# Memory's token tiles: turned by VectorE's block transposes and 128-byte stores, in place of TensorE

## What is computed

```python
h = rmsnorm(x, norm_mix_w)
gq, gk, gv, ggate, ga, dq, dk, dv, dgate = split_cols(h @ w_in)
o_gla = gla_chunked(gq, gk, gv, g)              # gated linear attention, 4 heads
o_diff = diff_attention(q, k, dv, lam)          # two softmax maps, 4 heads
x = x + concat(o_gla, o_diff) @ w_out
hc = rmsnorm(x, norm_cross_w)
mem_n = rmsnorm(mem, norm_mem_w)                # (256, 1024): the change is here
kv = mem_n @ w_ckv                              # keys and values of the memory
x = x + cross_attention(hc, kv, w_cq, w_co)
return rmsnorm(x, final_norm_w)
```

## Time and profile before

| | us |
|---|---|
| median of 3 runs | 816.72 |
| lowest to highest | 815.28 to 817.65 |
| the profiled execution's own time | 814.48 |
| its span, first to last instruction | 812.7 |
| TensorE busy in the span | 799.4 (98%) |
| VectorE busy | 593.1 (73%) |
| ScalarE busy | 422.1 (52%) |
| mean granted TensorE clock | 0.998 |

### The profile page before, as it was taken

How to read it: one execution, slowest core, us unless ns; L and a number is a source line. 1 busy time by engine, 2 the same in 40 slices (tenths; PEclk the granted TensorE clock), 3 DMA queues, 4 the chain that set the end, 5 groups by cost and what they waited for, 6 DMA issues and landing times.

```text
span 812.7 us, 13040 instructions
## 1 busy us (share of the span) xinstructions
PE 799.4 (98%) x4376; PEld 669.9 (82%) x4376; DVE 593.1 (73%) x1386; ACT 422.1 (52%) x1025; POOL 98.8 (12%) x138
## 2 busy tenths in 40 slices
PE   8999999999999999999999999999999999999996
PEld 7887888888788888888888798888888888888885
DVE  6688677675678678767868877798847563367997
ACT  7766445444455345445535556543645553366453
POOL 3100111121011010111212211010010000001201
PEclk9999999999999999999999999999999999999999
DMA  8331236568365334545667368954457312107945
GB/s 283 128 84 40 85 98 170 97 111 156 66 111 112 87 95 114 108 81 98 126 132 162 108 173 269 317 125 124 146 134 177 102 66 74 57 14 153 215 86 207
DMA packets 126538, 103.41 MB, mean 127 GB/s; under 512 B 58628, under 2 KB 96648, under 8 KB 126472
## 3 DMA queue, kind: packets, MB, share of 16 engines
q1 hardware_dynamic: 98184, 66.40, 28.2%
q0 software_dynamic: 15392, 29.36, 20.1%
q10 hardware_dynamic: 12896, 6.82, 2.9%
HBM read 85.77 MB, written 33.55 MB: 147 GB/s over the span
## 4 chain that ended last, share of the span: by engine, by line
PE 83%; DVE 9%; ACT 4%; issue 2%; DMA 1%; POOL 0%; ACTq 0%; DVEq 0%
PE bank L1936 14%; PE bank L1938 14%; PE bank L1937 14%; PE banks2to L1936 9%; PE banks2to L1938 9%; PE banks2to L1937 9%; PE banks2to L2193 3%; PE banks6to L1999 3%; PE bank L2216 2%; DVE w_lo L1442 2%; DVE neg_max L1738 1%; DVE actT_lo L1441 1%; PE banks2to L2133 1%; PE bank L2218 1%; PE banks2to L2120 1%
## 5 line engine op out<-in xcount | busy, mean ns | idle before, releaser
L1938 PE MATMUL bank<-w_hi,actT_lo 128*128 128x512 f32 x412 | 161.5, 392 | 0.0
L1936 PE MATMUL bank<-w_hi,actT_hi 128*128 128x512 f32 x384 | 154.6, 403 | 0.5 <-DVE memT_lo L1441 0.2
L1937 PE MATMUL bank<-w_lo,actT_hi 128*128 128x512 f32 x384 | 149.8, 390 | 0.0
L1442 DVE SCALAR_TENSOR_TENSOR w_lo<-w_raw,vecs,w_hi 128x512 fp32r<-128x512 f32 x120 | 87.0, 748 | 24.1 <-ACT w_hi L1158 23.8
L1938 PEld LDWEIGHTS bank<-w_hi,actT_lo 128*128 128x128 f32 x412 | 77.4, 188 | 16.9
L1158 ACT ACTIVATE w_hi<-w_raw,vecs 128x512 fp32r<-128x512 f32 x120 | 83.1, 721 | 14.3 <-DMA w_raw<-in_w_ckv 8.7
L1936 PEld LDWEIGHTS bank<-w_hi,actT_hi 128*128 128x128 f32 x384 | 72.2, 188 | 16.7 <-DVE w_lo L1442 1.6
L1937 PEld LDWEIGHTS bank<-w_lo,actT_hi 128*128 128x128 f32 x384 | 72.4, 188 | 13.1
L1030 POOL TENSOR_TENSOR rs_o<-var_o,neg_half 128x1 f32<-128x1 f32 (+1 forms) x48 | 31.1, 647 | 343.8 <-DVE var_o L1766 228.5
L1938 PE MATMUL banks2to<-w_hi,actT_lo 128*128 128x512 f32 x164 | 64.0, 390 | 0.0
L1325 ACT ACTIVATE prob<-banks2to,neg_maxs 128x128 f32<-128x128 f32 (+7 forms) x64 | 46.9, 740 | 15.2 <-DVE neg_maxs L1739 15.0
(11 more groups left out here) (377 smaller groups left out, 2037.6 us busy)
## 6 DMA issues: line engine op xcount, KB each, us to landing
w_raw<-in_w_in SPq DMA_DIRECT2D x56, 256.0 KB, 3.0
out_sums<-in_w_out POOLq DMA_DIRECT2D x11, 1024.0 KB, 9.0
late_sums<-in_w_co POOLq DMA_DIRECT2D x11, 1024.0 KB, 9.2
w_raw<-in_w_ckv SPq DMA_DIRECT2D x32, 256.0 KB, 3.6
w_raw<-in_w_cq SPq DMA_DIRECT2D x32, 256.0 KB, 2.9
stage_in<-in_x SPq DMA_DIRECT2D x8, 512.0 KB, 4.6
mixT<-mixed ACTq DMA_DIRECT2D x16, 256.0 KB, 4.0
x_res<-in_x SPq DMA_DIRECT2D x8, 512.0 KB, 5.7
```

The lines of the kernel that those rows point to most:

```text
L1442: return dve.scalar_tensor_tensor(dst, src, scale, hi.bitcast(F32), ALU.mult, ALU.subtract)
L1936: pe.matmul(dst, l_hi, r_hi, start=start, stop=False)
L1937: pe.matmul(dst, l_hi, r_lo, start=False, stop=False)
L1938: return pe.matmul(dst, l_lo, r_hi, start=False, stop=stop)
```

## The change

The memory tiles no longer go through TensorE. `scale` of tile 8+m now writes to another buffer, `stage_in` 2+m. In place of the two `tr` of the tile stands `mturn` m: one DVE transpose of 32x32 blocks over the whole 128x1024 tile, back to `stage_in` m. At the end of the gated steps 1 and 2, SP stores the tiles (`mstore`), four transfers of 32 partitions each, in runs of 128 bytes, to the scratch `memory_turned`. At the end of step 4 ACT issues two loads of it, one a tile, to `memT_lo` (`mback`). In the differential attention, behind `PV` of i = 8 (tile 0) and of i = 9 (tile 1), two stages `ms` each split half a tile: ACT copies to `memT_hi`, DVE subtracts in place in `memT_lo`. Waits that named `tr` of the memory tiles name `mturn` or the last tile of x; `Ka` waits for the splits.

```diff
-    plan += [*normed(TT + 1), ("G0", 1, 2), *tr(TT), ("w", 13), ("gsum", 1), ("gmid", 1), ("G0", 1, 3), ("w", 14)]
-    plan += [("G0", 1, 4), *tr(TT + 1), ("gexp", 1), ("w", 15), ("gdec", 1), ("G0", 1, 5), ("glaprep",), ("qk", 0)]
+    plan += [*normed(TT + 1), ("G0", 1, 2), ("mturn", 0), ("w", 13), ("gsum", 1), ("gmid", 1), ("G0", 1, 3), ("w", 14)]
+    plan += [("G0", 1, 4), ("mturn", 1), ("gexp", 1), ("w", 15), ("gdec", 1), ("G0", 1, 5), ("glaprep",), ("qk", 0)]
...
+        plan.extend([("mstore", s - 1)] if 1 <= s <= MT else [])
+        plan.extend([("mback", m) for m in range(MT)] if s == 4 else [])
...
             plan.append(("PV", i))
         plan.extend([("loadm", t - 6, 1)] if t >= 6 else [])
+        plan.extend([("ms", i - TT, kk) for kk in range(2)] if TT <= i < TT + MT else [])
...
+                elif kind == "mstore":
+                    m = w[0]
+                    sp.wait_ge(tr_dve, 2 * TT + m + 1)
+                    for band in range(P // BLK):
+                        rows = slice(BLK * band, BLK * band + BLK)
+                        tokens = slice(P * m + BLK * band, P * m + BLK * band + BLK)
+                        sp.dma_start(mem_turned[:, tokens].rearrange("(b r) c -> r b c", r=BLK),
+                                     stage_in[rows, m, :].rearrange("r (b c) -> r b c", c=BLK)
+                                     ).then_inc(d_stage[2 + m], 16)
...
+                elif kind == "mback":
+                    m = w[0]
+                    act.wait_ge(*memory_stored(m))
+                    act.dma_start(memT_lo[:, :, cols(m)].bitcast(F32),
+                                  mem_turned[:, cols(m)].rearrange("(k p) c -> p k c", p=P)).then_inc(d_stage[m], 16)
+                elif kind == "ms":
+                    hi, raw = memory_tile(*w)
+                    act.wait_ge(*memory_back(w[0]))
+                    copy(hi, raw.bitcast(F32)).then_inc(tr_act, 1)
...
                 elif kind == "scale":
                     t = w[0]
                     dve.wait_ge(rs_ok, at("sq", t))
-                    dve.tensor_scalar(stage_in[:, t % NSTAGE, :], stage_in[:, t % NSTAGE, :], rs_in[:, t:t + 1], None,
+                    to = t % NSTAGE if t < TT else t % NSTAGE + 2
+                    if t >= TT:
+                        dve.wait_ge(tr_pe, at("tr", t - 2, 1))
+                    dve.tensor_scalar(stage_in[:, to, :], stage_in[:, t % NSTAGE, :], rs_in[:, t:t + 1], None,
                                       ALU.mult).then_inc(scaled, 1)
...
+                elif kind == "mturn":
+                    m = w[0]
+                    dve.wait_ge(scaled, at("scale", TT + m))
+                    dve.transpose(stage_in[:, m, :], stage_in[:, 2 + m, :]).then_inc(tr_dve, 1)
+                elif kind == "ms":
+                    hi, lo = memory_tile(*w)
+                    dve.wait_ge(*memory_back(w[0]))
+                    dve.wait_ge(tr_act, memory_split(*w))
+                    lo_part(lo, lo.bitcast(F32), hi).then_inc(tr_dve, 1)
...
                     if s == 0:
-                        pe.wait_ge(tr_dve, at("tr", TT + 1, 1))
+                        pe.wait_ge(tr_dve, at("tr", TT - 1, 1))
```

More of the change, by code:

```diff
@@ L669, in build @@
         tile_a = sb("tile_a", [P, D])
+        mem_turned = nc.dram_tensor("memory_turned", (D, M), F32, kind="Internal").ap()
         mixed = nc.dram_tensor("mixed", (D, S), F32, kind="Internal").ap()
@@ L843, in input_dest, with memory_tile, memory_stored, memory_back @@
         def input_dest(t, kk):
-            hi, lo, c = (actT_hi, actT_lo, cols(t)) if t < TT else (memT_hi, memT_lo, cols(t - TT))
-            return hi[:, 4 * kk:4 * kk + 4, c], lo[:, 4 * kk:4 * kk + 4, c]
+            return actT_hi[:, 4 * kk:4 * kk + 4, cols(t)], actT_lo[:, 4 * kk:4 * kk + 4, cols(t)]
+        def memory_tile(m, kk):
+            k = slice(4 * kk, 4 * kk + 4)
+            return memT_hi[:, k, cols(m)], memT_lo[:, k, cols(m)]
+        def memory_stored(m):
+            return d_stage[2 + m], 16 * 2 + STORED
+        def memory_back(m):
+            return d_stage[m], 16 * 4
+        def memory_split(m, kk):
+            return 2 * TT + 2 * m + kk + 1
         def turned_rows(first, n, t, band):
@@ L1213, in _ @@
                         act.wait_ge(g0_dve, 4)
-                        act.wait_ge(tr_pe, at("tr", TT + 1, 1))
+                        act.wait_ge(tr_pe, at("tr", TT - 1, 1))
+                        act.wait_ge(tr_dve, 2 * TT + MT)
                     if s >= 2:
@@ L1573, in _ @@
                     dve.wait_ge(pool_c, 5)
-                    dve.wait_ge(tr_pe, at("tr", TT + 1, 1))
-                    dve.wait_ge(tr_act, at("tr", TT + 1, 1))
+                    dve.wait_ge(tr_pe, at("tr", TT - 1, 1))
+                    dve.wait_ge(tr_act, at("tr", TT - 1, 1))
+                    dve.wait_ge(tr_dve, 2 * TT + MT)
                     dve.wait_ge(z_pe, 2)
@@ L2018, in _ @@
                     if t % 2 and t > 3:
-                        pe.wait_ge(z_act, 1 + (t > TT))
+                        pe.wait_ge(z_act, 1)
                     for j in range(4):
@@ L2074, in _ @@
                         pe.wait_ge(g0_dve, 4)
-                        pe.wait_ge(tr_dve, at("tr", TT, 1))
+                        pe.wait_ge(tr_dve, at("tr", TT - 2, 1))
                     wait(pe, kd_dve, keys_turned(s) - 1)
@@ L2222, in _ @@
                     pe.wait_ge(pj_dve, GLA_STEPS + DIFF_STEPS)
+                    pe.wait_ge(tr_dve, memory_split(MT - 1, 1) + MT)
                     project(job, late_bank(job)[:, 0:M], weights(P * w[0]), memory_tokens(slice(0, M)), 0, 6)
```

## The result

The changed kernel takes 817.37 us (median of 20 runs, 815.65 to 820.95), the kernel before 815.91 us on the same chip (median of 20, 814.77 to 817.65). The ratio is 1.0023, with a 95% interval of 1.0014 to 1.0031. So the change costs about 1.9 us, between 1.1 and 2.5 (the two medians by themselves differ by 1.46). That is inside the 0.3% (2.45 us) that the prediction counts as no change, on its slow side.

The account below looks back on a forecast made before the run. The prediction took TensorE (98% busy) to bound the kernel, with DVE a second bound 0.18 us behind where memory is turned. Terms -0.20 (transposes), 0 (stores) and +1.25 (splits) gave +1.05 us: 816.72 to 817.8 us, range 815.0 to 820.3.

Parts of the forecast that it names:

- no change: Whole kernel: a difference within about 0.3% (2.45 us) cannot be told from none; chance given to this outcome 0.77.
- DVE as a second bound: Before steps 0 and 1: DVE stands 0.18 us behind TensorE, so 1.94 us taken off TensorE gains only 0.20.
- The rival in which all of the work counts: Whole kernel: all 1.94 us off TensorE is gained and the splits are hidden, giving 814.8 us; chance 0.13.
- The size of `mturn`: DVE's block transpose of 128x1024 in the memory stretch: 1185 ns, 1.12 us after overlap, extended from smaller rows.
- The stores: Turned tiles stored from about 96 and 99 us, landed by 107, before ACT asks at about 116: cost 0.
- the point from which the rival decides: Stores landing late, delaying ACT's queue at 116 us: from 2.2 times a packet's price; at three times 825.4 us; chance 0.05.
- The splits: Behind `PV` 8: DVE 2.29 us late, so `PV` 9 waits 1.45 us; net loss 1.25 us.
- Given back behind it: At `TQK` 12, after the `PV` 9 stop: TensorE's earlier 0.2 us wait for DVE's rotated keys comes back.
- The second pair: Splits behind `PV` 9: DVE 2.7 us late, `TQK` 12's lo part at 296.3, needed at 298.2 by `PV` 10: covered.
- The sum: Whole kernel: -0.20 + 0 + 1.25 = +1.05 us, median 816.72 to 817.8 us, +0.13%.
- both pairs of splits binding and weights late: Differential attention: 1.45 + 1.45 + 1 to 2 us lost with DMA traffic delaying weights, about 820.5 us; chance 0.12.
- the ends of the range: Whole kernel: 815.0 to 820.3 us, said to run from the first rival to the smaller of the slower ones.

Follow-up runs that it names:

- e3: The change, with the sine table, half of the gates of `G0e` 1 and `rope` moved behind the values and masked copy of step 0: 814.17 us, ratio 0.9981.
- e5: The kernel before, transposes still on TensorE, with only the new order of DVE's and ACT's work before step 0: 815.84 us, ratio 1.0002.
- e7: The change, with the splits of steps i = 8 and 9 moved from behind `PV` to behind `comb`, ahead of the projection: 815.66 us, ratio 1.0004.
- e1: The change, with the four splits moved: one half tile behind each `PV` of i = 10 to 13: 818.10 us, ratio 1.0033.
- e6: The change, with every memory tile stored twice, first to a scratch nobody reads, ACT waiting for both: 822.67 us, ratio 1.0079.
- e2: The change, with 16 useless transposes of the identity on TensorE, eight behind each `mturn`: 817.27 us, ratio 1.0018.
- e4: The change, with both the edits of e1 and of e3: 816.08 us, ratio 1.0002.
- e8: The change, with both the edits of e3 and of e7: 813.48 us, ratio 0.9973.
- e9: The change, with a useless DVE memset of 128x1024 before the lo part of the values of step 0: 819.52 us, ratio 1.0048.

## Why the prediction was right, and where it was not

**DVE as a second bound: right.** The forecast was 1.3 us of stop at `kv` 0, together 1.3 to 1.7 us, and a gain of 0.20 from the 1.94 us that left. The rows show 1.55 + 0.19 = 1.74 us of stop, a hair above the upper end, and a gain of 0.09 us (from -0.36 to -0.45 in the table). TensorE itself came a little earlier than forecast: it starts the first projection at 71.40 us, 8.86 behind `scale`, in place of 10.96 (73.86), so 2.10 us early and not 1.94. e3 and e5 show the mechanism from both sides: with DVE's order changed the gain is 2.2 us, and without the work taken from TensorE the order is worth nothing. The rival in which all of the work counts was right about a kernel with another order, and wrong about this one.

**The size of `mturn`: slightly low.** 1.185 us forecast by extension from 256 and 512 columns, 1.24 measured; 1.16 from start to start in place of 1.12. From `scale` to the end of the masked copy DVE gained 0.06 us (19.46 to 19.40), where 0.08 was forecast. The larger part of the missing gain is the signal from the masked copy to the turned key, 0.15 us (82.09 less 81.45 + 0.49) where 0.06 was taken: with it, only 0.03 us of TensorE's 0.18 behind DVE were slack.

**The stores: right in their cost, wrong in their times.** Nothing waits for them. But the second tile is stored from 104.4 us, not from 99, since a step lasts 7.3 us (116.45 - 109.13, the same copy one step apart, from ACT's timeline) and the stores of one step of outputs go out between. The cover was 5 us, not 9. And the point from which the rival decides was too far off: a packet at 2.2 times its price was named, while twice the number of stores gives ACT 5.59 us of idle time in place of 1.28.

**The splits: right in the mechanism at `PV` 9, and the equal hundredths are luck.** DVE's maxima are 2.35 us late in place of 2.29 (288.11 less 285.42 is 2.69, against 0.34 before). The forecast's 1.45 us was counted from start to start (290.58 less 289.13); the bracket's 1.45 us begins at the listed end of the matmul before. From start to start the loss is 1.61 us (from +1.45 at 255.27 us, behind the last older wait, to +3.06): 0.06 more from DVE, and 0.15 us for the signal (292.19 less 291.62 + 0.42) where 0.06 was taken. Given back behind it: 0.18, forecast 0.20. So the splits cost 1.43 us and not 1.25. The second pair binds nothing: the lo part of `TQK` 12 ends at 297.50 + 0.41 = 297.91, and `PV` 10 starts at 299.79, a slack of 1.9 us, as forecast. e7 shows that the price was one of place: the same splits ahead of DVE's idle time cost nothing that is seen in `PV` 9.

**What failed: a term that was not there.** The sum took a stop to cost its own length. In the profiled execution of the change the clock also falls behind the stop, which costs 1.6 us, and by their mean clock 7 of the 20 executions have such a fall. Their median is 819.12 us, that of the other 13 is 816.75, so this term is worth about 0.6 us on the median of 817.37; without it the medians would differ by 0.84 us, near the forecast of +1.05. That stop and fall belong together is shown by the counts, 18 of 53 against 1 of 131, and by the profiles: of the five kernels with the stop, three (the change, e1, e6) have the fall at 83 us, and none of the other six profiles has one there. Their price is not shown as well: e2, which has neither the stop nor the lower clock, came out no faster than the change by anything its interval can tell.

**Two sums of the rivals.** With both pairs of splits binding and weights late, the terms named (1.45 + 1.45 + 1 to 2) give 820.6 to 821.6 us on 816.72, where about 820.5 is written; and the ends of the range, 815.0 and 820.3, stand 0.2 us inside the rivals that they are said to run between. Neither touches the outcome.

**What stays open.** The waits for `w_ckv` near 480 to 510 us are 0.7 us before, 1.7 in the change, 2.2 in e1, 1.7 in e2, 0.5 in e3, 1.1 in e4, 0.7 in e5 and e7, 0.8 in e8, 1.0 in e6, 1.4 in e9. They follow neither edit. It may be that they depend on the time at which weight loads land beside other transfers; no run here tests that, and a single profile each doesn't settle it. Part of the differences between e2, e3 and e8 that the stops do not explain may lie there.

## What to carry to other kernels

Before work is taken from the busiest engine, follow the second engine's unbroken row of work to the point where they meet: if it ends within some tenths of a microsecond of the first (0.18 us here), the saving turns into a stop there, until the second engine's list is put in the order in which the first one needs it (here 0.1 us became 2.2). Put moved work directly ahead of an idle time of the engine that does it, not behind the work whose follower is urgent; in a list walked in order, a stage whose input is not ready costs its wait as well as its work (1.06 and 1.2 us here). And look at the granted clock behind every new stop, because a busy share doesn't show it.

## What the hardware showed that was not expected

The granted clock of TensorE fell from 2.4 to 1.2 GHz for some 3.4 us behind 1.74 us of stops in the profiled execution, and by the mean clocks in about a third of the executions of one and the same kernel. In e6 it fell for 6.8 us behind a stop of 1.61 us. Stops of 1.45 us before `PV` 9, and of 1.63 us in e1 at 326 us, were not followed by one in the profiled executions, and neither was the stop of 2.65 us in the profiled execution of e9, though the other four of its five executions show the lower mean. The Trainium skill, "TensorE: Matmul & The Clock Gate", Part 1, says that the number of slow matmuls differs from one run to the next of the same kernel, since the chip's own timing does not start with the kernel's; it says so of a kernel's start. No run here tests the reason; what the counts show is that the same kernel, with the same stop in its midst, has the fall in some executions and not in others.

Four stores in 128-byte runs (1024 runs each) hold SP's queue for 2.8 to 4.2 us, single ones for 0.45 to 2.5 us; in e6, where four more precede them or follow, four take 3.6 to 5.6 us. So the time for which stores hold the queue that issues them is of the size of their estimated price on the DMA engines, 4.6 us a tile, and belongs in the sum beside it.
